# A transformer block with a PEER feed-forward on one NeuronCore: the mixer in two passes by tokens, with the router's first part and 30 groups of gathers inside the second

## What is computed

```python
h = modulate(x, norm_mix_g, sh1, sc1)              # rms norm, shift and scale from c
q, latent, dq, dk, dv, gate_a, gate_b = mixer_front(h, pos, lw)
o_mla, o_dil, state = attend(...)                  # MLA (8 heads) and 3 dilated groups
y = gate_a * (o_mla @ w_branch_mla) + gate_b * (o_dil @ w_branch_dil)
x = x + gt1 * (y @ w_out)
h2 = modulate(x, norm_ffn_g, sh2, sc2)
# PEER: 8 heads; two halves of a query score 128 keys each; top 16 of each; 256 pair sums;
# top 16 pairs name 16 of 16384 experts, gates are a softmax of the pair sums
a = gelu(einsum('nd,nhkd->nhk', h2, expert_u[eidx])) * g
x = x + gt2 * einsum('nhk,nhkd->nd', a, expert_v[eidx])
```

## Time and profile before

| | us |
|---|---|
| median of 3 runs | 4468.44 |
| lowest and highest | 4434.17, 4475.28 |
| the profiled execution | 4437.73 |
| its span | 4435.9 |
| stage borders: ada and norm to 78.5, MLA projection to 272, MLA attention to 446, sample attention to 600, dilated groups to 1390, combine to 1515 | |
| mixer 1515.3 to 1951.0 | 435.7 |
| FFN before its dense phase 1951.0 to 2965.3 | 1014.3 |
| dense phase 2965.3 to 4436 | 1471 |

### The profile page before, as it was taken

One profiled execution on the slowest core, in us unless ns is written; L12 is line 12 of the kernel. 1 busy time (PEld: TensorE's weight loads), 2 busy tenths in 40 slices (PEclk: granted clock), 3 DMA queues, 4 the chain that ended last, 5 costly groups with the idle time before them and its releaser, 6 DMA issues.

```text
span 4435.9 us, 43263 instructions
## 1 busy us (share of the span) xinstructions
PE 3813.1 (86%) x14474; PEld 2492.2 (56%) x14474; DVE 2733.2 (62%) x6387; ACT 1199.5 (27%) x3231; POOL 861.9 (19%) x718
## 2 busy tenths in 40 slices
PE   7789879899994499977998767889999999899986
PEld 5458357788983388864444344435444445454443
DVE  1665544351344311237999997767779676976876
ACT  2346332331223211122222467621111111111111
POOL 0000000101000000001323223333333333343332
PEclk8889889897797699988999889999999999999998
DMA  4000200402113311125888789999999999999997
GB/s 153 5 2 1 55 38 22 136 29 88 55 53 133 120 43 43 67 102 218 307 323 332 300 315 368 382 418 414 412 395 381 414 412 406 373 400 413 393 354 290
DMA packets 256139, 1016.81 MB, mean 229 GB/s; under 512 B 28682, under 2 KB 103842, under 8 KB 170930
## 3 DMA queue, kind: packets, MB, share of 16 engines
q0 software_dynamic: 101520, 723.10, 41.1%
q1 hardware_dynamic: 131058, 280.39, 17.2%
q10 hardware_dynamic: 23344, 10.59, 0.9%
HBM read 964.74 MB, written 49.25 MB: 229 GB/s over the span
## 4 chain that ended last, share of the span: by engine, by line
PE 26%; DVE 14%; DMA 12%; ACT 2%; issue 2%; SPq 0%; POOL 0%; ACTq 0%; DVEq 0%
DMA ff_room<-in_v 9%; PE banks L2431 8%; PE banks L2417 8%; PE banks L2406 4%; DVE ff_rows L2080 4%; PE banks L2354 2%; DVE ff_acc L2046 2%; DMA gates_dram<-ff_room 1%; PE banks L2299 1%; DMA ff_rows<-in_uv,pk_expert 1%; DVE pk_eq L1736 1%; DVE pk_axes L1741 1%; DVE mx_x L2106 1%; PE banks L2378 1%; DVE pk_besti L1715 1%
## 5 line engine op out<-in xcount | busy, mean ns | idle before, releaser
L1978 POOL DMA_INDIRECT ff_rows<-in_uv,pk_expert x640 | 805.4, 1258 | 1507.4 <-DVE ff_acc L2046 825.6
L2080 DVE CUSTOM_DVE_ANT_0 ff_rows<-ff_rows,ff_h_row 128x1024 f32<-128x1024 f32 x648 | 766.5, 1220 | 45.0 <-DMA ff_rows<-in_uv,pk_expert 43.1
L2431 PE MATMUL banks<-ff_room,mx_x 128*128 128x512 f32 x1536 | 700.5, 607 | 58.3 <-DVE mx_x L2121 31.2
L2417 PE MATMUL banks<-mx_x,ff_room 128*128 128x384 f32 x2048 | 683.7, 487 | 10.8 <-ACT mx_x L2264 10.8
L2406 PE MATMUL banks<-ff_rows,o_mla_tops 128*128 128x512 f32 x904 | 443.9, 640 | 142.8 <-ACT o_mla_tops L2174 140.7
L2417 PEld LDWEIGHTS banks<-mx_x,ff_room 128*128 128x128 f32 x2048 | 389.5, 190 | 310.2 <-issue 73.6
L2431 PEld LDWEIGHTS banks<-ff_room,mx_x 128*128 128x128 f32 x1536 | 296.4, 194 | 418.5 <-issue 356.9
L2046 DVE SCALAR_TENSOR_TENSOR ff_acc<-ff_rows,ff_a,ff_acc 128x1024 f32<-128x1024 f32 x388 | 498.6, 1285 | 7.2
L2406 PEld LDWEIGHTS banks<-ff_rows,o_mla_tops 128*128 128x128 f32 x904 | 178.2, 205 | 359.0 <-issue 195.3
L176 PE MATMUL banks<-d_w_high,h_high 128*128 128x512 f32 (+1 forms) x648 | 276.6, 427 | 30.9 <-DVE d_w_low L183 30.0
L2162 ACT ACTIVATE ff_gelu<-ff_dots 128x2 f32<-128x2 f32 x324 | 65.6, 203 | 828.7 <-DVE ff_dots L2080 828.5
(11 more groups left out here) (390 smaller groups left out, 5828.2 us busy)
## 6 DMA issues: line engine op xcount, KB each, us to landing
ff_room<-in_uT SPq DMA_DIRECT2D x128, 512.0 KB, 14.8
ff_room<-in_v SPq DMA_DIRECT2D x128, 512.0 KB, 22.0
gates_dram<-ff_room SPq DMA_DIRECT2D x6, 4096.0 KB, 16.8
mx_x<-gates_dram SPq DMA_DIRECT2D x128, 192.0 KB, 17.0
d_w<-in_w_dil POOLq DMA_DIRECT2D x9, 2048.0 KB, 8.0
d_w<-in_w_ada POOLq DMA_DIRECT2D x32, 512.0 KB, 4.8
ff_room<-in_w_pq SPq DMA_DIRECT2D x32, 512.0 KB, 4.4
ff_rows<-in_uv,pk_expert POOLq DMA_INDIRECT x640, 10.8
```

Of the source, the lines that this page charges most:

```text
L1978: pool.indirect_dma_start(out=rows[r][:, :], out_offset=None, in_=IN["uv"][:, :], in_offset=bass.IndirectOffsetOnAxis(ap=at, axis=0))\
L2080: ins = dve.tensor_tensor_reduce(rows[r][:, 0:D], rows[r][:, 0:D], h_row[i % 2][:], 1.0, 0.0, ALU.mult, ALU.add, dots[:, B % RB, j:j + 1])
L2417: ins = pe.matmul(SD[:, 0:ND], u[e % 4][:, k, :], hd[:, k, :], start=(k == 0), stop=(k == KD - 1))
L2431: ins = pe.matmul(Y[j][:, half], ad[e % 2][:, j * P:(j + 1) * P], v[e % 4][:, half_rows[half]], start=(e == 0), stop=(e == NK - 1))
```

## The change

**Front.** The weights of the MLA projection (five), and those of the sample attention with the page table, get buffers of their own and are issued by SP at the end of its queue in `stage_ada_and_norm`. The weights of the first dilated group are issued by POOL during the sample attention. The squares are summed two tiles at a time, at n = 3, 5, 7, 9. Of the eight final activations ACT keeps three; DVE makes five. In the MLA projection, PE projects two tiles ahead and transposes queries and keys of the tile before; queries have three buffers, keys and squares two, latents and statistics four; ACT copies the queries' transposes.

**Mixer.** The tokens are taken in two passes: 0 to 255 alone, then 256 to 1031 in two parts of 388. A sub-unit is one gate with its branch; there are 16 in pass 1 and 32 in pass 2, over three pairs of PSUM banks; y is made in two steps. Each pass loads and splits all weights. After pass 1's output its norm is made, and h2 of the first two tiles is written. After the second sub-unit of pass 2 the router for these tiles runs (16 queries, scores, top 16), and DVE makes tile 0's picks (parts 0 and 1 there, 2 to 4 in slots 2 to 4). POOL gathers tile 0's first 30 batches into two buffers of two rows; DVE's dots and sums and ACT's gelus for them stand in slots of pass 2 and of its output.

**FFN.** It has no first router, no picks of tile 0, and begins with batch 30 of tile 0, so 98 batches stand before the dense phase. POOL stores the rows of the other tiles after the first ten gathers. `ON_VEC`, `PICK0`, `HOT0`, `HOTS` and `PIECES` are set anew.

The diff, cut to its core:

```diff
@@ stage_ada_and_norm
+                for m in range(2):
+                    sp.dma_start(c.w_q[:, m], IN["w_q"][m]).then_inc(c.mla_in, 16)
+                for dst, src in ((c.w_kv, "w_kv"), (c.w_uq, "w_uq"), (c.w_uk, "w_uk"), (c.w_uv, "w_uv")):
+                    sp.dma_start(dst[:], IN[src]).then_inc(c.mla_in, 16)
+                for dst, src in ((c.w_ukT, "w_ukT"), (c.own_key, "diag"), (c.table, "page_table")):
+                    sp.dma_start(dst[:], IN[src]).then_inc(c.mla_sample_in, 16)
...
-                    if 4 <= n < 4 + KD:
-                        squares_sum(n - 4)
+                    if n in (3, 5, 7, 9):
+                        squares_sum(n - 3)
+                        squares_sum(n - 2)
@@ stage_mla_project, PE
                 project(0)
+                project(1)
                 for t, (t0, n) in enumerate(TILES):
...
+                    if t:
+                        turn_q(t - 1)
...
-                    if t + 1 < len(TILES):
-                        project(t + 1)
-                    turn_heads(t, kf, s["kT_mm"], s["kT_copy"], s["k_fin"])
-                    turn_heads(t, qs, s["qT_mm"], s["qT_copy"], s["q_fin"])
+                    if t + 2 < NT:
+                        project(t + 2)
+                    if t:
+                        turn_k(t - 1)
@@ stage_mix
+    NB, RB = MIX_BATCHES, 2
+    ROUTER_AT = 1
+    BATCH_AT = [z for z in range(5, 32) if z % 6 != 4] + list(range(33, 48, 2))
+    batch_at = {z: b for b, z in enumerate(BATCH_AT[0:NB])}
...
+            def _(pool):
+                pool.wait_ge(s["half_tile"], 1)
+                for b in range(NB):
+                    if b >= RB:
+                        pool.wait_ge(s["rsum"], (b - RB + 1) * G)
+                    for j in range(G):
...
+                        pool.indirect_dma_start(out=ring[:, r, :], out_offset=None, in_=IN["uv"][:, :],
...
+                def dot(b):
+                    if b >= RB:
+                        dve.wait_ge(s["a"], b - RB + 1)
+                    for j in range(G):
+                        dve.wait_ge(rows_in[r], 16 * (b // RB + 1))
+                        ins = dve.tensor_tensor_reduce(u, u, h_row, 1.0, 0.0, ALU.mult, ALU.add, dots[:, b % RB, j:j + 1])
...
+                def background(z):
+                    if z in batch_at:
+                        b = batch_at[z]
+                        dot(b)
+                        if b:
+                            sums(b - 1)
...
+                for z in range(len(SUBS) - S1):
+                    mixed(S1 + z)
+                    for n in made_after(S1 + z):
+                        w_low(dve, n)
+                    if z == ROUTER_AT:
+                        for hp in range(HP):
+                            dve.wait_ge(s["sc_copy"], hp + 1)
+                            for part in range(4):
+                                top16(part, hp)
...
+                        picks(0)
+                        picks(1)
+                    if 2 <= z <= 4:
+                        picks(z)
+                    background(z)
@@ stage_ffn
-    ORDER = [0, 1] + DENSE + [2, 3, 4, NT - 1]
+    ORDER = [1] + DENSE + [2, 3, 4, NT - 1]
-    PICK0, HOT0, HOTS = HP * LATE_PER + 3, HP * LATE_PER + 13, 2
+    PICK0, HOT0, HOTS = HP * LATE_PER + 3, HP * LATE_PER + 10, 3
-    TURN0 = 112
+    TURN0 = 86
-    ON_VEC = list(range(LATE_PER, HP * LATE_PER, LATE_PER))
+    ON_VEC = list(range(LATE_PER, first[1] - 1, LATE_PER))
...
+                    if B == RB:
+                        store_rows()
```

More of the change, by code:

```diff
@@ new lines, in root, with turned @@
+                def root(t, ss, out, ready, done):
+                    n = TILES[t][1]
+                    act.wait_ge(ready, t + 1)
+                    act.activation(out[0:n], ss[0:n], ACT.Sqrt, scale=1.0 / QK, bias=c.eps[0:n]).then_inc(done, 1)
+                def turned(t, mm, dst, done):
+                    t0, n = TILES[t]
+                    for half, bank in ((0, X0), (1, X1)):
+                        act.wait_ge(mm, 2 * t + half + 1)
+                        act.activation(dst[:, half * HB:(half + 1) * HB, :],
+                                       bank[0:QK, :].rearrange("p (h q) -> p h q", q=P)[:, :, 0:n],
+                                       ACT.Copy).then_inc(done, 1)
@@ L1506, in stage_mix @@
         ts = sb("ts", [P, KD, NSA])
[L1507 to L1511 removed]
+        dots, act_of, a = (sb(t, [P, RB, G]) for t in ("dots", "gelu", "a"))
@@ new lines, in stage_mix @@
+        pk = Picks(c, ctx, [0], "px_", [c.expert0], [c.gate0],
+                   [c.x_normed[:, at:at + PH // 2, 0:NE] for at in (0, PH // 2)])
+        acc, h_row = c.acc0, c.o_mlaT[:, :, 0:NE]
+        s = {n: c.sem("mx_" + n) for n in ("w_hi w_lo mm sig y y_hi y_lo out_mm out stored sq sum root inv xn h2 "
+                                           "keys_in q_mm q_copy sc_mm sc_copy top h_mm h_copy half_tile "
+                                           "dot gelu a rsum").split()}
+        gs, sh = c.gs[:, 1], c.mod[:, 3]
@@ new lines, in residual, with keep @@
+                def residual(p):
+                    for k in range(KD):
+                        sp.dma_start(x[:, k, own(p)], IN["xT"][:, k, own(p)]).then_inc(x_in[k], 16)
+                def keep(p):
+                    for m in range(KD):
+                        sp.wait_ge(s["out"], m + 1 if p == 0 else O1 + 2 * (m + 1))
+                        sp.dma_start(c.dram["x1_dram"][:, m, own(p)], x[:, m, own(p)]).then_inc(s["stored"], 16)
+                for m in range(KD):
+                    branch(m)
+                    weight(2 * m)
+                    weight(2 * m + 1)
+                    if m == 2:
+                        sp.dma_start(keys, IN["keysT"]).then_inc(s["keys_in"], 16)
+                    if m == 3:
+                        queries(0)
+                        queries(1)
@@ new lines, in _ @@
+                for n in range(S1, S1 + 4):
+                    weight(n)
+                sp.wait_ge(s["mm"], S1)
+                residual(0)
+                for n in range(S1 + 4, W1):
+                    weight(n)
+                branch(KD)
+                branch(KD + 1)
+                weight(W1)
+                weight(W1 + 1)
+                keep(0)
+                weight(W1 + 2)
+                for n in range(2, HP):
+                    queries(n)
+                weight(W1 + 3)
@@ new lines, in scores @@
+                def scores(n):
+                    pe.wait_ge(s["q_copy"], n + 1)
+                    if n:
+                        pe.wait_ge(s["sc_copy"], n)
+                    for t in range(EARLY):
+                        ins = pe.matmul(S[:, t * NK:(t + 1) * NK], qT[n % 2][:, t * P:(t + 1) * P], keys[:, n, :],
+                                        start=True, stop=True)
+                    ins.then_inc(s["sc_mm"], 1)
+                for u in range(S1):
+                    gated(u)
@@ new lines, in _ @@
+                y_high(1)
+                w_high(act, W1 + 2 * KD + 1)
+                for m in range(KD):
+                    for n in made_beside(1, m):
+                        if n > W1 + 2 * KD + 1:
+                            w_high(act, n)
+                    for i in range(2):
+                        if 32 + 2 * m + i in batch_at:
+                            weights(batch_at[32 + 2 * m + i])
+                    squares(1, m)
+                roots(1)
+                modulate(1, slice(NE, NPR))
@@ new lines, in sums @@
+                def sums(b):
+                    dve.wait_ge(s["a"], b + 1)
+                    for j in range(G):
+                        v, weight = ring[:, b % RB * G + j, D:2 * D], a[:, b % RB, j:j + 1]
+                        if b == 0 and j == 0:
+                            ins = dve.tensor_scalar(acc, v, weight, None, ALU.mult)
+                        else:
+                            dve.wait_ge(s["rsum"], b * G + j)
+                            ins = dve.scalar_tensor_tensor(out=acc, in0=v, scalar=weight, in1=acc, op0=ALU.mult, op1=ALU.add)
+                        ins.then_inc(s["rsum"], 1)
@@ L2070, in _ @@
                 for B, (i, b) in enumerate(batches):
-                    if b == 0 and i < 2:
-                        dve.wait_ge(s["h_copy"], NS - 2 + i + 1)
+                    if B in first[0:2]:
+                        dve.wait_ge(s["h_copy"], NS if i else 1)
                     elif b == 0:
@@ L2403, in _ @@
                             r = B % RB * G + j
-                            ends = dict(start=(b == 0 and j == 0), stop=(B + 1 == first[i + 1] and j == G - 1))
+                            ends = dict(start=(B in first[0:ON_PE] and j == 0), stop=(B + 1 == first[i + 1] and j == G - 1))
                             for half in range(2):
```

925 lines of the change are left out of this document (566 added, 359 removed).

## The result

| | before | changed |
|---|---|---|
| median of 21 runs each | 4435.74 | 4465.99 |
| lowest, highest | 4396.25, 4475.28 | 4437.89, 4483.45 |
| ratio, 95% interval | | 1.0066 [1.0047, 1.0085] |

The change makes the kernel 0.7% slower. The three runs shown of the kernel before had a median of 4468; over 21 it is 4436, within 2 us of the profiled execution of before (4437.73). The changed kernel's first profiled execution is the lowest of its 21 (4437.89).

The account below looks back on a forecast made before the run. It saw a chain of waits with no single owner, the mixer being TensorE's. Front -63, mixer +205 and FFN -170 summed to -28: 4410 from the profiled execution, 4440 from the median, halfway 4425; range 4355 to 4510 us.

Parts of the forecast that it names:

- the period P of the loop: Mixer pass 2 and output: gather, dot and sums form a closed loop of 12.9 us per batch, 27 loops, 348 us.
- (d): FFN one-hots and gates: 32 batches at three quads instead of 48 at two, gate-write cycle 53 us from 58.9, -35.
- rival B: Mixer loop longer: landing 10.8 us, period 15.9, +81, total 4506 us; chance 0.25.
- Rival D: FFN gives back less: gate cycle stays (+35), late periods TensorE-bound (+15), total 4475 us, no change; chance 0.12.
- (a) to (c) and (e): FFN before its dense phase: earlier start -86, late router +15, earlier picks and one-hots -10, remaining DMA-full batches -54.
- Front, -63: Stages before the mixer: ada -8, MLA weights -10, MLA projection -35, preloads -2 and -8; from -75 to -40.
- Two passes by themselves: Mixer: the pure TensorE work of 16 short and 32 longer sub-units plus output takes nothing more than now.
- Mixer up to the loop, 255 us: Mixer start: pass 1 and two sub-units 129 us, router to 203, first gather 220, first dot over at 255.
- The sum: Whole kernel: -63 + 205 - 170 = -28 us; a batch moved into the mixer costs 6.8 us and gives back 5.7.
- The base: Starting time: profiled execution 4437.7 us, median of runs 4468.4; the forecast was put halfway between the two resulting times.
- Rival A: Mixer pass 2: batches land within a slot and TensorE's 6.86 us sets the pace, -86, total 4340 us; chance 0.12.
- Rival C: Mixer pass 2: TensorE's clock falls to 1.2 GHz, a sub-unit takes 13.7 us, +99, total 4524 us; chance 0.07.

Follow-up runs that it names:

- the exchange of two lines: The changed kernel with VectorE's sums of the batch before put ahead of the new batch's dot in each mixer slot: 4362.16 us, ratio 0.9799.
- front alone: The change's front stages, with mixer, picks and FFN of the kernel before: 4368.12 us, ratio 0.9823 to the kernel before.
- 15 in the mixer: The changed kernel with 15 batches in the mixer instead of 30 and two quads of one-hots to a batch instead of three: 4387.8 us, ratio 0.9887.
- the two passes alone: The changed front and two-pass mixer without router, picks and gathers in it, with the FFN of the kernel before: 4366.63 us, ratio 0.9806.
- the sigmoid first: The kernel with sums ahead of the dot, and ScalarE's sigmoid of a slot ahead of the gelu of the slot before: 4338.57 us, ratio 0.9804.

## Why the prediction was wrong

It had the change 28 us faster by its sum, and the traces have it 26 slower. Two terms failed: the period P of the loop, whose landing was taken too short (30 us over its 27 turns), and (d), the one-hot phase (24 us). The first had the right mechanism and the wrong size. The second rested on a wrong reading: that more quads to a batch would quicken the phase. The measured 4466 lies within the stated range, but the change went the other way.

- **The loop, P = 12.9.** The mechanism was right, closed by two buffers and the order dot, sums; the exchange of two lines shows it. The term that failed is its landing, "its second row lands 1.26 + 7.8 us later". 7.8 was a median over first and second rows alike, and the loop waits for the second: over the turns above its mean is 8.6, while the first row's median is 5.6. With the 0.27 us from sums to issue, that makes 13.8 in the gated part, 20 us over its 21 loops. In the output phase a pair took 14.5 us (dots from 2003.8 to 2090.9, six loops), with its two rows issued 2.0 us apart and not 1.26: 10 more. The step between the two parts took 17.9 (18 forecast). So 30 of the mixer's 33 us are the loop. My rival B had P = 15.9, with the gain gone from 13.9: the loop stood right at that point.
- **FFN, (d), -35.** This failed: "part of a cycle is the slow pace of two quads". The phase from the first one-hot to the last write went from 364.6 to 353.2 us, -11, and the writes of gates are 56.8 us apart where I took 53 and it was 58.9. At two quads it hid 48 batches, at three 32, and 16 batches more or less in it changed it by only 18 us (front alone) to 30 us (15 in the mixer against the changed kernel). Rival D had this (the gate cycle stays, "gate writes 55 apart still"), its sign came true, and I gave it 0.12.
- **FFN, (a) to (c) and (e).** F+83 for the first step's end (80 forecast), +22 for the late router (+15), -7 for picks (-10), -66 for the rest (-54). Right in kind; that the last is 12 us better than forecast hides half of (d)'s miss, by luck.
- **Front, -63.** Measured -76 in the traces and -72 alone. ada and the weights' preload -19.7 (18 forecast), the projection -43 more (35), sample and dilated preloads -9 (10). The period came to 9.5 where I took 10.5: I had held TensorE's work to 11.0 at the clock of that window and gone a little under it. Here the window of the latents has a granted clock of 1.00, with TensorE busy for 92%, where it was 0.83 at 73%. These 13 us more also made the miss smaller than it was.
- **Two passes by themselves, nothing more than now.** Right, within 2 us.
- **Mixer up to the loop, 255 us.** Right: in the first trace the router's last matmul is 200 us after the mixer's start (203 forecast), the first gather 225 (220), the first dots are over at 253.
- **The sum.** I had priced a moved batch at 6.8 against 5.7, with router and picks mixed in. The batches alone are 5.0 against 4.9. Router and picks cost 88 us in the mixer, and the 85 that they free at the FFN's start are lost again behind the one-hot phase, because the raised `HOTS` puts 16 more batches there at 5 us each. Of the 148 us that the 30 moved batches give back, some 80 (16 x 5, an estimate) thus only undo what three quads had cost. My sum counted the batches left behind the phase rightly (8), and never asked what two quads would give. All 30 batches in the mixer at two quads were not run.
- **The base.** Halfway between the profiled execution and a median of three (4453) was too high by 17 us; the median of 21 is 4436, near the profiled execution. The forecast of 4425 looks nearer to 4466 for that than its sum was.
- Rival A (latency hidden) describes not this kernel but the ones with sums first: they take 4362 and, with the sigmoid first, 4339, where A had 4340. Rival C: the clock fell to 0.84 at 68% busy, as the rows had said for such a share, and the loop covered it. The dense phase is 9 us longer here and 5 in the front alone, where its code is that of before, but not in the two passes alone (1470.2, with the same code); I leave that open.

The Trainium skill's rule to issue early and wait late ("DMA: Bandwidth & Descriptors", section "Rules for kernel authors") is what the exchanged lines do. The runs agree: it was worth 104 us here.

## What to carry to other kernels

When work is moved under another stage, ask of both ends what it costs there. A phase whose length its batches don't set (here the one-hot phase) holds them for 1 to 2 us each, and behind it they cost 5. A change that lowers how many it hides loses again what the move won. A ring of two buffers is a closed loop of latency if the release of one buffer is queued behind the wait for the other; put the release first. When you add up such a loop, take the landing of the transfer that it waits for last, not a median over all transfers.

## What the runs showed of the hardware

- Gathers of 1 MB issued by GpSimd in pairs 1.24 us apart, one pair each 13.8 us at a DMA share of 0.50, landed after a median of 5.6 us (the first of a pair) and a mean of 8.6 us (the second), each from its own issue.
- The same stages with the same instructions took 698 us at a granted clock of 0.92 and 729 at 0.88, in two executions of one kernel.
- Loading 16 MB of weights and splitting 12 MB of them a second time, beside a TensorE that is 94% busy, cost 1 to 2 us of 429.
- With two functions in turn on ScalarE, each turn brought two table loads of 1.28 us. In a loop of 13.8 us they stood beside waits; once that loop was opened, the order of the two functions on the queue was worth 21 us.
